# First block's attention: where the gate products stand between softmax steps, when the first weight tile is split, and the last query block's scores in pairs

## What is computed

```python
def block(i):                       # one query block of 128 rows, i = 0..3
    logits = jnp.einsum('bqhd,bsd->bqsh', qib, k_idx_f)
    score = jnp.einsum('bqsh,bqh->bqs', jax.nn.relu(logits), wib)
    score = jnp.where(causal[None], score, -jnp.inf)
    _, idx = lax.top_k(score, topk)             # 128 keys for each query
    s = jnp.einsum('bqngd,bqknd->bngqk', qg, k_sel) * (HEAD_DIM ** -0.5)
    p = jax.nn.softmax(jnp.where(valid, s, -jnp.inf), axis=-1)
    return jnp.einsum('bngqk,bqknd->bqngd', p, v_sel)
...
g = jax.nn.sigmoid(gates)           # gates: 3072 of the columns of h @ w_in
merged = g[:, :, 0] * y_pool + g[:, :, 1] * y_conv + g[:, :, 2] * y_attn
```

## Time and profile before

| | |
|---|---|
| median of 3 runs | 3141.71 us (3139.44 to 3145.6) |
| the profiled execution, its own time | 3142.27 us |
| span of that execution in the profile | 3140.5 us |
| PE busy over the span | 2822.4 us (90%) |
| DVE, ACT, POOL busy | 1834.6, 1153.8, 1023.0 us |
| PE's mean granted clock | 0.944 of full speed |
| `attention` in the first layer | 213.3 to 371.9 us of the span |
| `attention` in the second layer | 1058.3 to 1218.8 us |

### The profile page before, as it was taken

The page is one execution under the profiler, slowest core; times in us unless marked ns, Lnnn a source line. Parts: engine busy times, 40 slices in busy tenths (PEclk is TensorE's granted clock), DMA queues, the critical chain, the costliest instruction groups (busy, mean ns, idle before and its releaser), DMA issues. The chain is left out here.

```text
span 3140.5 us, 59085 instructions
## 1 busy us (share of the span) xinstructions
PE 2822.4 (90%) x25000; PEld 2224.9 (71%) x25000; DVE 1834.6 (58%) x2779; ACT 1153.8 (37%) x2127; POOL 1023.0 (33%) x582
## 2 busy tenths in 40 slices
PE   7999798999989998999999799978888887699987
PEld 4765576877867655767778587857777775479875
DVE  5878656886059786478840456466666644353062
ACT  4234434333142344343321522234455533332252
POOL 1422142544423211334444222244444430142202
PEclk8999999999999989999999899989999988799988
DMA  6322133433323211244332323220000004133111
GB/s 214 90 78 54 35 94 96 141 119 88 96 82 93 69 47 48 81 134 144 114 89 86 122 84 99 86 70 23 4 23 23 24 8 148 32 99 91 54 38 54
DMA packets 350230, 249.42 MB, mean 79 GB/s; under 512 B 10874, under 2 KB 322448, under 8 KB 349456
## 3 DMA queue, kind: packets, MB, share of 16 engines
q1 hardware_dynamic: 342704, 229.62, 24.2%
q10 hardware_dynamic: 7264, 16.03, 1.6%
HBM read 221.59 MB, written 16.52 MB: 76 GB/s over the span
## 5 line engine op out<-in xcount | busy, mean ns | idle before, releaser
L540 POOL TENSOR_TENSOR weights_lo<-weights_raw,weights_hi 128x1024 fp32r<-128x1024 f32 (+2 forms) x230 | 581.5, 2529 | 1114.5 <-ACT weights_hi L509 1114.5
L1179 PE MATMUL psum<-moving_hi,weights_hi 128*128 128x512 f32 x1472 | 601.6, 409 | 40.8 <-PEq L178 13.7
L1179 PE MATMUL psum<-moving_lo,weights_hi 128*128 128x512 f32 x1472 | 581.2, 395 | 0.0
L1179 PE MATMUL psum<-moving_hi,weights_lo 128*128 128x512 f32 x1472 | 580.7, 394 | 0.0
L1179 PEld LDWEIGHTS psum<-moving_hi,weights_hi 128*128 128x128 f32 x1472 | 280.7, 191 | 161.1 <-issue 68.0
L509 ACT ACTIVATE weights_hi<-weights_raw 128x1024 fp32r<-128x1024 f32 (+1 forms) x240 | 248.3, 1036 | 249.5 <-PE psum L1179 244.7
L1179 PEld LDWEIGHTS psum<-moving_hi,weights_lo 128*128 128x128 f32 x1472 | 280.8, 191 | 60.9
L1179 PEld LDWEIGHTS psum<-moving_lo,weights_hi 128*128 128x128 f32 x1472 | 281.8, 191 | 56.0 <-issue 3.8
L2596 POOL TENSOR_TENSOR second_off<-second_mats,second_masks 128x256 f32<-128x256 f32 x180 | 140.7, 786 | 154.8 <-PE psum L2059 154.1
L2652 PE MATMUL psum<-hn_hi,even_hi 128*128 128x256 f32 x480 | 166.4, 347 | 8.6 <-DVE hn_lo L1996 7.7
L2652 PE MATMUL psum<-hn_lo,even_hi 128*128 128x256 f32 x480 | 164.1, 342 | 0.0
(11 more groups left out here) (470 smaller groups left out, 6122.4 us busy)
## 6 DMA issues: line engine op xcount, KB each, us to landing
weights_raw<-in_w_up SPq DMA_DIRECT2D x88, 512.0 KB, 3.7
weights_raw<-in_w_in SPq DMA_DIRECT2D x80, 512.0 KB, 3.6
ada<-in_ada_w SPq DMA_DIRECT2D x9, 2048.0 KB, 9.4
odd_raw<-in_od_w_in SPq DMA_DIRECT2D x16, 1024.0 KB, 5.5
even_raw<-in_ev_w_in SPq DMA_DIRECT2D x30, 512.0 KB, 3.9
weights_raw<-in_w_down SPq DMA_DIRECT2D x32, 448.0 KB, 3.6
weights_raw<-in_w_o SPq DMA_DIRECT2D x16, 512.0 KB, 3.8
weights_raw<-in_w_down SPq DMA_DIRECT2D x16, 512.0 KB, 3.8
```

Source lines behind the costliest of these rows:

```text
L540: ops.tensor_tensor(self.ring.lo[i % n][:, a:b], self.ring.raw[:, t % self.ring.landing, a:b], self.ring.hi[i % n][:, a:b].bitcast(F32), A ...
L1179: return nc.tensor.matmul(to, (hi, lo)[which][:, at:at + P], moving(k)[part], start=start and k == 0 and i == 0, stop=stop and k == n_k - ...
```

## The change

It does three things, all in `attention`, and so in both layers.

1. **The products are dealt out by a table for each block.** `GATES_BESIDE[b]` names the products in the pick, beside each of the 8 heads, and in the 3 ends. In the picks there are now 12, 17 and 26 (before 20, 28, 32), beside the heads of the four blocks 8, 8, 5 and 4 (before 8 each), and in the ends 6, 8, 9 and 9 (before 0). The sum stays 112.
2. **The first two tiles are split one by one.** ACT makes the first high part as its first instruction of the stage and the second after the second exponential; DVE makes the first low part ahead of the first `weigh`, and the second ahead of the second `weigh`.
3. **In the last block, scores are made for two heads at a time**, and go to four banks in turn (0 to 3), of which the logits, finished by then, used two. The waits follow.

```diff
-PARTS_WHILE_PICKING = (0, 20, 28, 32)
+GATES_BESIDE = (([0], [1] * HEADS, [2, 2, 2]),
+                ([12], [1] * HEADS, [2, 3, 3]),
+                ([17], [1, 1, 0, 1, 1, 0, 1, 0], [3, 3, 3]),
+                ([26], [1, 0, 1, 0, 1, 0, 1, 0], [3, 3, 3]))
...
-            count = PARTS_WHILE_PICKING[b] if h < 0 else 1 if h < HEADS else 0
+            picking, by_head, last_turns = GATES_BESIDE[b]
+            count = (by_head + last_turns + picking)[h]
...
-            score_bank = lambda n, width: bank(n % 2, width)
+            score_bank = lambda n, width: bank(n % 2 if n < (QB - 1) * HEADS else n % 4, width)
...
-                    if n >= 2:
+                    if b + 1 == QB and h in (2, 3):
+                        pe.wait_ge(logits_taken, n - 3)
+                    elif b + 1 == QB and h >= 4:
+                        pe.wait_ge(scores_taken, n - 3)
+                    elif n >= 2:
                         pe.wait_ge(scores_taken, n - 1)
...
                 def ahead_of(b, h):
-                    scores(b, h)
                     if b + 1 < QB:
+                        scores(b, h)
                         logits(b + 1, h)
+                    elif h % 2 == 0:
+                        scores(b, h)
+                        scores(b, h + 1)
...
+                s.split_hi(act, 0)
                 for b, h in places:
...
-                    if (b, h) == (0, 0):
-                        for i in range(ring.split):
-                            s.split_hi(act, i)
+                    if b == 0 and 1 <= h < ring.split:
+                        s.split_hi(act, h)
...
                             peak(b, h)
+                            if b == 0 and h < ring.split:
+                                s.make_lo(dve, nc.vector, h, s.first_lo_done)
                             if b + 1 < QB:
                                 weigh(b + 1, h)
-                        if (b, h) == (0, 0):
-                            s.split_first(dve)
```

## The result

The changed kernel takes 3103.14 us (median of 4 runs, 3100.23 to 3106.2), the kernel before 3140.57 beside it (4 runs, 3130.54 to 3145.6). The medians lie 37.4 us apart. The ratio of the runs is 0.9883, with a 95% interval of 0.9868 to 0.9899, which is 36.7 us. The forecast was 3107 in a range of 3092 to 3128. The profiled execution took 3106.2 us, with a span of 3104.4.

What follows compares the result with a forecast made beforehand. The stage was taken as bound by DVE in the picks and by PE, with waits, elsewhere. Terms of -16.9 us (first layer) and -18.0 (second), together -34.9 from 3142.27, gave 3107 us, range 3092 to 3128.

Steps and rivals of the forecast that it cites:

- Block 0: Block 0: first product 2.9 us earlier, more if the clock holds; -4.5 us in the first layer, -2.3 in the second.
- The further 3.3: Block 0: three heads that went slowly could give up to 3.3 us more if the clock holds.
- Pick 1 and block 1: First pick and following block: first `weigh` without waits -2.9 us, stall moved to last head +0.5; -2.4 a layer.
- the clock in the new gaps: Ends of picks 1 and 2: PE without work lowers its clock; +1.7 us a layer, ends 0 and +5.0.
- Pick 2 and block 2: Second pick and following block: earlier first `weigh` -6.9 us, 0.6 given back, three fewer products -2.0; -8.3 a layer.
- The 0.6 given back for a held mask: Pick 2 and block 2: a POOL split ending about with the pick can hold the mask; 0.6 us given back.
- Pick 3 and block 3: Third pick and last block: products +5.4 us, pairs -4.2, waits -3.7, clock gain; -3.4 first layer, -6.7 second.
- rival A: Splits fall on masks, norms and first pick steps: three more 2.2 us stalls a layer, +13 us, 3120; chance 0.14.
- The picks' clock: Pick 3: PE no longer rests, so its clock loss goes; -1.7 us in the first layer, 5.0 in the second.
- B: Block 3: ACT and DVE pace heads, pairs give nothing, nine products lengthen end; +8.4 us, 3115 or more; chance 0.12.
- C: Blocks 1 to 3: PE at 1.2 GHz for 48 heads, +53 us, 3157; decides from 35 slow heads; chance 0.06.
- D: Block 0, picks 1 and 2: first tile not landed, something but products sets first `weigh`; -10.7 us left, 3132; chance 0.08.

Runs made afterwards that it cites:

- the second execution: The changed kernel run again without any edit, on another chip: 3103.33 us, ratio 0.9882 to the kernel before.
- the kernel with products moved: Changed kernel with products moved from the last block: pick 1 15 for 12, pick 2 18 for 17, last block 6 and 1, 1, 1: 3099.32 us.

## Why the prediction was right, and where it was not

*Block 0* (-4.5 and -2.3; measured -4.1 and -1.7). The first product starts where the sum put it, 2.35 us after the stage's start for a predicted 2.2. The further 3.3 were to come if the clock held, and it didn't (0.82 in both layers). How far it falls is not the order's doing alone: with one and the same order in block 0, the changed kernel and the run with 15 products in pick 1 took 17.05, 18.5 or 21.58 us there, at clocks of 0.90, 0.82 and 0.68.

*Pick 1 and block 1* (-2.4 in each layer; measured -0.5 in the first, -0.9 in the second). This is the step that was mis-sized. Its mechanism is there: the first `weigh` came at once and took 0.41. The stall did move to the last head, as the step said; PE waits 1.76 us behind it for 0.56 without it, so it may have cost nearer 1.2 than the 0.5 charged. What was left out is that the new gap of 2.02 us stands right ahead of this block, and that the clock often falls there (in 8 of the 12 traced layers with this gap, and in none of the 6 in which 15 products fill it): the charge of +1.7 for "the clock in the new gaps" was put on the stage as a whole and was this block's. Where the clock happened to stay at 1.00 (18.31 us in place of 19.86), the block gains 2.3 against the 20.65 that the kernel before took at 1.00 in the first layer; less the 0.3 that pick 1 grew, that is 2.0 of the 2.4.

*Pick 2 and block 2* (-8.3; measured -8.0 and -8.8). Right, with its parts: the first `weigh` is 0.48 us long and starts 0.9 after the pick. The 0.6 given back for a held mask wasn't needed; the mask took 0.36.

*Pick 3 and block 3* (-3.4 and -6.7; measured -3.9 and -6.8). Right in sum, not in its parts. The text said that the picks would not move, and pick 3 grew by 2.2: a split lies over its first step (2.50 us), which is rival A's mechanism. It cost nothing that the trace shows, because PE was still at work on products and has no wait for DVE behind it. The pairs gave 4.5 and 5.5 alone and 3.1 on top of the table, for 4.2. That the nine products of the last ends lie open is right, and where in the block they stand is worth 0.4 a layer.

*The picks' clock.* The sum took a gain from the clock only in pick 3. It rose in all three picks of the first layer, from 0.90, 0.92 and 0.93 to 1.00. An estimate of what that was worth: block 1 lost 4.63 us with 0.78 in place of 1.00, that is with 2 x 0.22 x 22.94 = 10.1 us at the lower of the two levels (0.50 and 1.00), 0.46 us for each. Summed over the blocks, the stage before spent 20.7 and 27.4 us at that level, and after 10.3 in each layer: up to 4.8 and 7.9 us of the 16.5 and 18.2, fewer where DVE sets the pace. So it is in part luck that the sum came within 0.4 us of each layer's gain: another execution of the same kernel had 145.4 and 139.15 us in its two layers. Of the signs that the prediction named, the stage's 142 us and block 2's 15 came in both layers, and the clock of 0.97 over the stage didn't quite (0.96).

*The rivals.* A: two stalls of 2.5 us remain of three. One may have cost PE some 1.2 us, the other nothing that shows; three more of 2.2 a layer did not come. B: the pairs pay, and so do the ends of blocks 0 to 2. In the last block it has a point: with the ends emptied block 3 is 1.7 and 0.3 us shorter, though by far less than the 4.2 it asked for. C: block 1 shows the mechanism (in the second execution 3.16 us from one head's product to the next in the first layer, 1.74 in the second) for some heads, not for the 35 that it needed; it cost block 1 up to 4.6 us in a layer. D: the first tile had landed and the products did set the first `weigh`; each part does what it says.

## What to carry to other kernels

Read first which engine is still behind at the end of the stage: here PE was, and what counted was less work on it (the pairs) and work moved into its idle gaps (ends of blocks, ends of picks, the stage's start). Before a stall on another engine is moved, look for the wait on PE that stands behind it, and afterwards for new ones: here moving the stalls spared PE 2.6 us of waits, and a new wait and the clock took them back. Fill such a gap with what fits into it, one product for a wait of 0.78 us and three for 2.02, and take them from the stretch where PE has no gap. Before an edit is credited with a few us, compare the same block in two layers and two executions: here one order gave 35.4 and 41.5 us at different clocks.

## What the runs showed of the hardware

- The clock fell behind short gaps. After 1.04 us between two stages, 0.9 us of small matmuls and 1.43 of waiting, the first product ran at 1.2 GHz in the first layer of the changed kernel (0.80 us), and behind the same gaps at 2.4 GHz in the first layer of the run with empty ends (0.50 us). With the second gap filled, PE stayed at 2.4 GHz in both layers. Behind the one gap of 2.02 us at the end of pick 1 the clock of block 1 was below 1.00 in 8 of 12 layers. "TensorE: Matmul & The Clock Gate" in the Trainium skill, "Why this matters for your kernels", asks for no long gaps between bursts; in these rows it fell behind short ones too, not every time.
- Once down, it stayed down for up to 17 us with PE busy 24.27 of 25.70 us. What brings it back these runs don't settle.
- A POOL split holds some DVE steps for its whole length and others not at all. The add at the start of a pick (L1135, two inputs) took 2.50 us, `weigh` 2.44 to 2.47, and the mask (L1140) 2.5 in the kernel with products moved; the searches and removals of pick 2 (384 columns) stayed at 0.54 to 0.56 us beside a split. The Trainium skill, "SBUF — State Buffer", section "Who interferes with whom", says that DVE steps with two inputs in SBUF, and one-input forms such as `tensor_scalar` where they run in a two-port mode, contend with GpSimd, and other one-input steps don't; the trace agrees, 2.50 us against 0.54.
- Three matmuls of 64 rows and 512 columns that all use the same half of the array took 2.73 us, 0.9 each, while two on different halves take 1.13 together.
